# One 4 MB weight piece loaded in ten row-strided transfers instead of one

## What is computed

```python
def moe_ffn(h, w_router, b_router, w_gate_up, b_gate_up, w_down, b_down):
    ...
    def expert_block(args):
        tok, e = args
        hgu = xt[tok] @ w_gate_up[e] + b_gate_up[e]
        gate = jnp.minimum(hgu[:, 0::2], SWIGLU_LIMIT)
        up = jnp.clip(hgu[:, 1::2], -SWIGLU_LIMIT, SWIGLU_LIMIT)
        act = gate * jax.nn.sigmoid(SWIGLU_ALPHA * gate) * (up + 1.0)
        return act @ w_down[e] + b_down[e]
```

## Time and profile before

| | |
|---|---|
| median of three runs | 1242.45 us |
| the profiled execution's own time | 1242.62 us |
| its span, first to last instruction | 1240.8 us |
| TensorE busy | 1194.2 us, 96% |
| DMA read from HBM | 445.09 MB, 360 GB/s over the span |

### The profile page before, as it was taken

How to read it: one execution, slowest core, us unless ns; L and a number is a source line. 1 busy time by engine, 2 the same in 40 slices (tenths; PEclk the granted TensorE clock), 3 DMA queues, 4 the chain that set the end, 5 groups by cost and what they waited for, 6 DMA issues and landing times.

```text
span 1240.8 us, 16272 instructions
## 1 busy us (share of the span) xinstructions
PE 1194.2 (96%) x7262; PEld 570.5 (46%) x7262; DVE 293.4 (24%) x646; ACT 188.3 (15%) x360; POOL 7.8 (1%) x18
## 2 busy tenths in 40 slices
PE   7999999999999999999998989999999989999997
PEld 5788578875543333434333333333343334333332
DVE  2156454443321111211111111111121111111111
ACT  3363212234110100000000000000000000000102
POOL 0000000000000000000000000000000000000000
PEclk9999999999999999999999999899999999999999
DMA  8332655349899999999999999999999999999995
GB/s 299 121 134 75 214 178 170 120 152 406 346 409 428 426 429 428 426 436 428 433 432 432 428 433 427 434 430 432 431 430 433 429 433 428 432 429 433 426 427 219
DMA packets 37228, 448.31 MB, mean 361 GB/s; under 512 B 11632, under 2 KB 11904, under 8 KB 18592
## 3 DMA queue, kind: packets, MB, share of 16 engines
q1 hardware_dynamic: 26928, 440.36, 84.7%
q10 hardware_dynamic: 9040, 3.01, 1.0%
q0 software_dynamic: 1184, 3.82, 1.0%
HBM read 445.09 MB, written 2.10 MB: 360 GB/s over the span
## 4 chain that ended last, share of the span: by engine, by line
PE 74%; DMA 24%; DVE 1%; issue 0%; ACT 0%; DVEq 0%; ACTq 0%; SPq 0%
PE ps L1663 27%; DMA ring<-w_gate_up 21%; PE ps L1688 9%; PE ps L1261 8%; PE ps L1352 7%; PE ps L1642 4%; PE ps L1717 4%; DMA ring<-w_down 3%; PE ps L1339 2%; PE ps L1537 2%; PE ps L1671 2%; PE ps L1707 1%; PE ps L1698 1%; PE ps L1291 1%; PE ps L1602 1%; DMA consts<-cst 1%
## 5 line engine op out<-in xcount | busy, mean ns | idle before, releaser
L1663 PE MATMUL ps<-ring,xacc 128*64 128x512 f32 x2048 | 466.7, 602 | 19.9 <-DMA ring<-w_gate_up 19.8
L1663 PEld LDWEIGHTS ps<-ring,xacc 128*64 128x64 f32 x2048 | 142.4, 137 | 308.3 <-issue 301.9
L1688 PE MATMUL ps<-ring,aT 128*64 128x512 f32 x992 | 219.8, 595 | 7.2 <-DMA ring<-w_down 7.2
L1688 PEld LDWEIGHTS ps<-ring,aT 128*64 128x64 f32 x992 | 73.8, 138 | 149.2 <-issue 149.2
L1213 DVE TENSOR_SCALAR gc<-ps 128x512 f32<-128x512 f32 x32 | 22.1, 692 | 389.9 <-PE ps L1663 389.9
L1261 PE MATMUL ps<-hT,wbuf 128*128 128x256 f32 (+1 forms) x432 | 100.4, 391 | 0.8 <-DVE hT L850 0.8
L1156 DVE TENSOR_TENSOR xacc<-ps,consts 128x512 f32<-128x512 f32 x30 | 20.7, 691 | 336.8 <-PE ps L1642 336.8
L1261 PEld LDWEIGHTS ps<-hT,wbuf 128*128 128x128 f32 (+1 forms) x432 | 81.6, 192 | 18.3 <-issue 5.0
L1352 PE MATMUL ps<-hT,wbuf 128*128 128x256 f32 x384 | 85.6, 382 | 0.0
L1352 PEld LDWEIGHTS ps<-hT,wbuf 128*128 128x128 f32 x384 | 72.2, 190 | 11.3 <-issue 1.8
L809 ACT ACTIVATE sgm<-gc 128x512 f32<-128x512 f32 x32 | 20.2, 630 | 361.9 <-DVE gc L1213 361.9
(11 more groups left out here) (252 smaller groups left out, 682.5 us busy)
## 6 DMA issues: line engine op xcount, KB each, us to landing
ring<-w_gate_up SPq DMA_DIRECT2D x44, 4096.0 KB, 37.2
ring<-w_down SPq DMA_DIRECT2D x22, 4096.0 KB, 34.7
ring<-w_gate_up SPq DMA_DIRECT2D x38, 2048.0 KB, 16.5
ring<-w_down SPq DMA_DIRECT2D x17, 2048.0 KB, 19.3
wbuf<-w_in SPq DMA_DIRECT2D x25, 512.0 KB, 3.4
wbuf<-w_in SPq DMA_DIRECT2D x12, 1024.0 KB, 5.6
ring<-w_down SPq DMA_DIRECT2D x6, 1024.0 KB, 34.3
wbuf<-w_in SPq DMA_DIRECT2D x2, 2048.0 KB, 8.4
```

What stands on the lines that cost most here:

```text
L1663: last = mm(bank(GU_BANK + q, 0, 512, slice(64 * half, 64 * half + 64)), x_, w[:, :, half, :], start=k == 0, stop=k == KT - 1, skip_group_ ...
L1688: last = mm(bank(b, 0, 512, slice(64 * half, 64 * half + 64)), turned[:, c0:c0 + SLOTS], w[:, D * r + 512 * half:D * r + 512 * (half + 1)] ...
```

## The change

Piece 87 (`UNEVEN = PIECES - 9`) is loaded by a new function. The bytes and the destination are the same. It now comes in ten transfers, each of which takes a few whole rows (a row is one partition's 32 KB):

- `first` = 0 to 5: six transfers of 16 rows, the rows first, first + 8, first + 16 and so on up to first + 120.
- `first` = 6 and 7: two transfers of 8 rows each, one on the partitions 0 to 63 (first, first + 8, ...) and one on 64 to 127.

A transfer of 16 rows is meant to give one row to each of the 16 DMA engines, and one of 8 rows to give one to each of the lower eight. By that count a lower engine carries ten of the piece's rows and an upper one six, where the single transfer gave eight to each.

```diff
+        UNEVEN = PIECES - 9
...
-            return ((0, 4), (4, 8)) if n < IN_HALVES else ((0, 8),)
+            return ((0, 4), (4, 8)) if n < IN_HALVES else ((0, 8),) * (10 if n == UNEVEN else 1)
...
+            def load_rows(n):
+
+                for first in range(8):
+                    for lo in (0,) if first < 6 else (0, P // 2):
+                        rows = slice(lo + first, P if first < 6 else lo + P // 2, 8)
+                        sp.dma_start(ring[slot_of(n)][rows, :], pieces[n][rows, :]).then_inc(ring_full[slot_of(n)], 16)
...
                         if n in TAIL_PARTS:
                             load_tail(n)
+                        elif n == UNEVEN:
+                            load_rows(n)
                         else:
                             load(n, 0, PIECE, ring_full[slot_of(n)])
```

## The result

The changed kernel takes 1262.45 us in the median of four runs (1260.57 to 1262.91) against 1242.06 (1239.61 to 1242.78): a ratio of 1.0159 with a 95% interval of 1.0146 to 1.0171, so 20 us slower. I had forecast 1250.0 us and a range of 1240.4 to 1256. The direction was right and the size was not: 7.6 us forecast, 20 measured.

A forecast was written before the change was run, and what follows sets the result against it. It took weight loads by DMA to set the pace, with TensorE close behind; 0 (issues) + 0 (semaphores) + 7.6 us (late landings) gave 1250.0 us, with an 8-in-10 range of 1240.4 to 1256.

The forecast's parts named there:

- What bounds the kernel: Weight loads set the pace, TensorE follows closely; in the tail a landing later by d moves the end by d.
- that piece 87 can't move the start of expert 29: Expert 29 begins at 1138.85 us after waiting for piece 86; piece 87 and what follows can't move that.
- pieces 87 to 91 have slack: TensorE doesn't wait for these pieces, so lateness there costs nothing before the tail.
- The ceiling of 1.80 us for a gain: Earlier landings in the tail help by 1.80 us at most; then TensorE's own work is next.
- Issues and semaphores at 0: Ten issues by SP take some 4.6 us, covered by 10.8; semaphore steps add 0, at most 0.3 us.
- Time per row, a factor of 2: Strided rows of piece 87 take 2.43 us, not 1.216: lower engines lose 14.6 us, upper ones 4.9.
- My 7.6 us: Lateness of the tail's landings, 14.6 - 7.0, taken as the whole loss.
- The lead of 7.0 us: At the queue's end eight engines finish 7.0 us early; if these are the lower eight, it offsets their loss.
- A: Rival: handover works, rows keep 1.216 us, lower eight are ahead; 1240.65 us, chance 0.14.
- B: Rival: the six 16-row transfers stay in their engines' own groups, only lent rows collide; 1242.4 us, chance 0.23.
- C: Rival: lower eight engines are late; 1244.9 us with factor 1 (chance 0.08), 1257.0 with factor 2 (0.10).
- What the profile should show: Rate 215 to 350 GB/s from about 1138 to 1165 us, later weight waits of 1.8 + 7.6, end step below 7 us.

The follow-up runs named there:

- e12: Kernel before, but only the first half of each row of piece 87 loaded, in one transfer for all 128 partitions: 1239.85 us, ratio 0.9975.
- e7: Kernel before, piece 87's second half-rows only for partitions 0 to 63, in eight transfers of eight rows, stride four; rest of that half left out: 1241.74 us.
- e10: Kernel before, with piece 87 in four transfers of 32 rows, stride four, nothing left out: 1244.00 us against 1241.88.
- e2: The changed kernel with the same destination rows, but each of the ten transfers reads consecutive rows of HBM: 1264.14 us.
- e4: Kernel before, with piece 87 in two transfers of 64 rows, the even and the odd rows: 1242.69 us against 1242.21.
- e5: Kernel before, with piece 87 in two transfers, partitions 0 to 63 and then 64 to 127: 1260.04 us.
- e6: Kernel before, last quarter of piece 87's rows in 16 transfers of eight rows, stride four, all for the lower eight engines; the rest in one: 1250.01 us.
- e1: Kernel before, with piece 87 in eight transfers of 16 rows, stride eight, no rows lent: 1259.47 us.
- e3: Kernel before, with piece 87 in eight transfers of 16 neighbouring rows: 1262.42 us.
- e11: Kernel before, last eighth of piece 87's rows in eight transfers of 16 rows, stride eight; the rest in one, no rows lent: 1245.55 us.
- e13: The same kernel as e7, timed again in ten runs beside the kernel before: 1241.45 us, ratio 0.9997.

## Why the prediction was wrong

*What bounds the kernel.* Right for the tail, where landings pass to the end in full (20.0 us at piece 94, 20.3 in the span). Wrong ahead of it: that piece 87 can't move the start of expert 29, which came 7.6 us later, and that pieces 87 to 91 have slack, where TensorE waited 8.54 us for 87 and 1.25 for 89. The ceiling of 1.80 us for a gain was a little low: e12, with every engine 4.86 us earlier, is 2.0 to 4.3 us faster by its interval, and TensorE has no wait for weights left in the tail.

*Issues and semaphores at 0.* Right for the issues, though they took 6.27 us and not 4.6: back to back they are 0.66 us apart and not 0.47. e7's eight transfers and e10's four show that small transfers as such don't dip. Semaphore steps weren't measured apart.

*Time per row, a factor of 2.* The factor was right: 223 GB/s in the dip, 2.4 to 2.6 us for a row at its full depth, and e2 with e4 and e5 shows that it lies in where the rows are written. The step that failed is the next: I applied it to the strided rows alone, so that a lower engine would lose 14.6 us and an upper one 4.9. The dip takes every row that any engine moves, from about the first strided row to the last, 37 us. The lead then doesn't help, since the engines that are ahead slow the others on piece 86. The stretch of the earlier trace rows already showed it: the total fell to 208 of 415 GB/s although most of what moved there, between 14 and 20 us, was SP's, whose transfers span all partitions (packets, MB, share):

```profile
q1 hardware_dynamic: 322, 1.16, 69.0%
q0 software_dynamic: 160, 0.52, 34.5%
```

I read the row for its factor and not for its reach. My 7.6 us are also the lateness of expert 29's start; that is chance, since the one was worked out for the tail.

*The lead of 7.0 us.* I took the groups that stop early and late for the lower and the upper eight engines, in one order or the other. They are neither. The three late engines among the lower eight got two rows more, 2.43 us, and they set the last landings. The sums bear this out. Over the whole 80 us from 1120 to 1200 the rate falls from 427 GB/s before to 332 after:

```profile
1120.00:1200.00 80.00, 75.98 (x366) 27.56 (x364) 11.79 (x20) 5.64 (x10) 0.00 (x0) 0.98 1.00 427
1120.00:1200.00 80.00, 59.17 (x278) 21.99 (x276) 8.32 (x14) 4.42 (x8) 0.00 (x0) 0.87 1.00 332
```

That is 80 x (1 - 332 / 427) = 17.8 us of the 20.4 measured and leaves 2.6. The same sum leaves 3.4 us in e2 (328 GB/s) and 2.5 in e6 (398), the other two with lent rows, and 0.2 to 0.9 us in the runs without them: e1 (336), e3 (324), e5 (336) and e11 (409). So the lent rows cost about 2 to 3 us of their own, in keeping with the 2.43. It is still inferred: no run has a handover without a collision. The shorter windows shown with the experiments cut off the ends of the dip and don't close like this.

*The rivals.* A and B both need rows with a stride of eight at full speed, which e1 excludes, and e6 excludes lent rows at full speed. C came closest with its factor of 2 and 1257.0 us, still some 5 us too low, and for the wrong reason: it too slowed the strided rows alone, and the late engines are only in part the lower ones. A's premise was false too: e13 gives the upper engines twice the relief of the change, burdens nobody, and gains nothing that can be measured.

*What the profile should show.* The dip, the waits after 1165 us and groups that stop closer together all came. The waits summed to 12.2 us and not to 9.4, and 8.54 of them were for piece 87 itself; the 10.64 us at 1146.43 weren't forecast. The dip was deeper than most of my 215 to 350 GB/s and 37 us long where I had put it at 27, from 1138 to 1165.

## What to carry to other kernels

While a DMA queue is the pace, keep each weight transfer on all 128 partitions, or cut it along the row (the tail's halves and quarters ran at 419 GB/s), or by rows with a stride of two or four over all partitions (429 in e4 and e10). In this kernel transfers of one half, of 16 neighbours or of every eighth row took all 16 engines to about half rate for as long as they ran. Before rows are handed from late engines to early ones, test which engines are late by leaving out a part for one half of the partitions: if the last landing doesn't move, no handover away from that half can pay. A lent row is also written where its owner is writing; in e6, with a stride that cost nothing in e7, that brought the dip back.

## What was not expected of the hardware

A collision slows engines that have no part in it, those still on piece 86 among them, and to much the same rate in each pattern: 199 GB/s with 16 neighbours, 211 with a stride of eight, 223 with a half of the partitions. Why the others are held back stays open, and so does whether sharing a group is what counts, or writing outside one's own.

The waits have a second price. After 8.54 us of idling the 16 matmuls at 1169.69 took 5.58 us; 16 matmuls of that shape take 3.65 elsewhere, as at 1213.14. The granted clock there is 0.50 of full speed, that is 1.2 GHz, and it is back at 1.00 from 1176 us on (the column after the busy times):

```profile
1162.00:1169.00 7.00, 0.00 (x0) 0.00 (x0) 0.00 (x0) 0.00 (x0) 0.00 (x0) 0.60 0.94 276
1169.00:1173.00 4.00, 3.31 (x8) 1.01 (x10) 0.00 (x0) 0.00 (x0) 0.00 (x0) 0.50 0.97 418
1173.00:1176.00 3.00, 3.00 (x17) 1.33 (x14) 0.00 (x0) 0.00 (x0) 0.00 (x0) 0.90 1.04 448
1176.00:1190.00 14.00, 12.75 (x66) 4.99 (x66) 4.16 (x7) 1.23 (x2) 0.00 (x0) 1.00 1.00 428
```

These 1.9 us don't reach the end, since TensorE waits again at 1188.95 for a landing. In e10 they do, because its wait lies in the tail. A short wait has this price at one time and not at another. In the kernel before, 2.63 us of waiting ahead of 1138.85 were followed by eight matmuls in 3.52 us; in e10 2.62 us in the same place were followed by eight in 1.94. The window of before, with a granted clock of 0.56, and the row of e10:

```profile
1138.80:1141.00 2.20, 2.15 (x6) 0.82 (x8) 0.00 (x0) 0.00 (x0) 0.00 (x0) 0.56 1.04 447
```

```profile
1138.82 1.94 PE L1672 MATMUL ps<-ring,xacc 128*64 128x512 f32 x8 [2.62 <-DMA ring<-w_gate_up]
```

So times of single runs of this kernel that lie 1 to 2 us apart say little about the transfers.
